# First output stage of a two-block kernel: three of its four pairs by seven block products in place of eight

## The reference, cut to what matters

```
D_MODEL, SEQ, CTX_LEN = 1024, 512, 256          # float32 throughout

def hybrid_layer(x, ctx, mod, mod_c, rot, params, need_ctx_out):
    ...
    rw_l, _ = rwkv_branch(...)                   # [1, 512, 512], recurrent half
    ...
    o = block_attention(q, ...)
    mla_l = o * jax.nn.silu(g_mla)               # [1, 512, 512], attention half
    x = x + gate * (jnp.concatenate([rw_l, mla_l], axis=-1) @ w_out)     # 512x1024 @ 1024x1024
    ...

def first_block(...):
    ...
        x, ctx = hybrid_layer(...)
    return rms_norm(x, final_g)
```

## Time and profile before

| what | us |
|---|---|
| three timed executions | 2710.06, 2714.54, 2714.43 |
| their median | 2714.43 |
| the profiled execution | 2711.91 |
| its span | 2710.1 |
| TensorE busy in the span | 2577.2 (95%) |
| VectorE busy | 1684.0 (62%) |
| ScalarE busy | 948.3 (35%) |
| GpSimd busy | 841.4 (31%) |
| the stage, from its first matmul to the next stage's first | 745.39 to 826.73 |

### The profile page before, as it was taken

How to read it: one execution, slowest core, us unless ns; L and a number is a source line. 1 busy time by engine, 2 the same in 40 slices (tenths; PEclk the granted TensorE clock), 3 DMA queues, 4 the chain that set the end, 5 groups by cost and what they waited for, 6 DMA issues and landing times. The chain is left out here.

```text
span 2710.1 us, 59371 instructions
## 1 busy us (share of the span) xinstructions
PE 2577.2 (95%) x24556; PEld 2048.3 (76%) x24556; DVE 1684.0 (62%) x3037; ACT 948.3 (35%) x2174; POOL 841.4 (31%) x1083
## 2 busy tenths in 40 slices
PE   7989999999999999999999989999999899999998
PEld 5977788775645888867788867767888677858886
DVE  5656767764527837764652358659833776577675
ACT  2013424324422226632121259231212675122571
POOL 3323434330024510012233125236531444246010
PEclk9999999999999999999999999999999999999999
DMA  6331100112431114203101161121111311122200
GB/s 247 98 110 43 45 19 3 51 37 94 157 116 54 63 46 158 95 1 111 62 33 63 63 230 40 76 85 63 42 53 63 140 64 63 63 85 94 79 2 32
DMA packets 108460, 205.98 MB, mean 76 GB/s; under 512 B 21955, under 2 KB 26194, under 8 KB 107680
## 3 DMA queue, kind: packets, MB, share of 16 engines
q1 hardware_dynamic: 107920, 201.30, 21.3%
q0 software_dynamic: 272, 0.89, 0.1%
HBM read 186.85 MB, written 15.54 MB: 75 GB/s over the span
## 5 line engine op out<-in xcount | busy, mean ns | idle before, releaser
L739 PE MATMUL psum<-weights,h_t 128*128 128x256 f32 x1488 | 354.0, 381 | 5.5 <-ACT early_work L828 5.5
L739 PEld LDWEIGHTS psum<-weights,h_t 128*128 128x128 f32 x1488 | 280.1, 191 | 45.4 <-ACT early_work L828 6.7
L739 PE MATMUL psum<-z_l,x_tiles 128*128 128x256 f32 x816 | 192.8, 379 | 0.5 <-POOL z_l L954 0.5
L1528 DVE TENSOR_REDUCE neg_max<-psum 128x1 f32<-128x768 f32 x160 | 147.1, 955 | 67.1 <-PE psum L1304 57.1
L839 ACT ACTIVATE early_work<-psum 128x512 f32<-128x512 f32 (+1 forms) x80 | 45.0, 566 | 364.1 <-DVE psum L1112 248.0
L739 PEld LDWEIGHTS psum<-z_l,x_tiles 128*128 128x128 f32 x816 | 155.0, 190 | 21.9 <-issue 0.9
L1477 ACT ACTIVATE prob<-psum,neg_max 128x768 f32<-128x768 f32 x128 | 114.2, 897 | 79.2 <-DVE neg_max L1528 79.2
L1112 DVE TENSOR_TENSOR psum<-psum,early_work 128x512 f32<-128x512 f32 x62 | 43.1, 696 | 144.6 <-PE psum L739 144.6
L1600 POOL TENSOR_TENSOR z_l<-z_l,inv_total 128x128 f32<-128x128 f32 x64 | 25.4, 401 | 308.6 <-DVE inv_total L1536 308.6
L739 PE MATMUL psum<-weights,x_tiles 128*128 128x256 f32 x496 | 117.2, 379 | 0.0
L790 PE MATMUL psum<-weights,h_t 128*128 128x512 f32 x256 | 111.5, 593 | 1.2 <-PEq L240 1.2
(11 more groups left out here) (548 smaller groups left out, 6674.2 us busy)
## 6 DMA issues: line engine op xcount, KB each, us to landing
weights<-in_ada_w_dram SPq DMA_DIRECT2D x30, 2048.0 KB, 8.0
weights<-in_a_w_in_dram SPq DMA_DIRECT2D x10, 2048.0 KB, 8.1
weights<-in_b_w_in_dram SPq DMA_DIRECT2D x8, 2048.0 KB, 8.0
weights<-in_c_w_in_dram SPq DMA_DIRECT2D x8, 2048.0 KB, 8.1
weights<-in_w_in_dram SPq DMA_DIRECT2D x6, 2048.0 KB, 8.8
x_aside<-x_tiles SPq DMA_DIRECT2D x24, 512.0 KB, 2.6
x_tiles<-x_aside SPq DMA_DIRECT2D x4, 3072.0 KB, 15.7
weights<-in_a_w_out_dram SPq DMA_DIRECT2D x4, 2048.0 KB, 8.2
```

Of the source, the lines that this page charges most:

```text
L739: last = pe.matmul(dst, lhs[:, k, :], rhs[k // 2][:, k % 2, :], start=k == 0, stop=k == KH - 1)
L1528: dve.tensor_reduce(neg_max[:, i % 4, m:m + 1], score_at(i, m), AX, ALU.max, negate=True)\
```

## The change

The diff, cut. `homes` are the places for the right sums and the partial results; the left sums get a new local buffer.

```
-def out_norm_stage(pr, tiles, m_t, bias_col, g_col, next_bank, columns=False, ctx_2=False):
+def out_norm_stage(pr, tiles, m_t, bias_col, g_col, next_bank, homes, columns=False, ctx_2=False):
...
+    half_pairs = n // 2
+    pairs = [(c, p) for c in range(2) for p in range(half_pairs)]
...
+        left = local("left_sums", [P, half_pairs, 4, KT // 2, P])
+        sevens = out_sevens(pr, tiles, m_t, (left,) + homes)
...TensorE
-            for c in range(2):
-                w = pr.weights.get(pe)
-                for i, t in enumerate(tiles):
...
-                    if c == 0 and 1 <= i <= early:
-                        flip(i - 1)
-                    if c == 1 and i:
-                        flip(early + i - 1)
+            for x, (c, p) in enumerate(pairs):
+                if x == 0:
...                        (two tiles by eight steps of 128x512 each, as before)
+                elif p:
+                    first = early + 2 * p - 2 if c else 2 * p - 2
+                    sevens.products(pe, c, p, w, beside=lambda at: flip(first + at))
+                else:
+                    sevens.products(pe, c, p, w)
...
-                if x == 0:
-                    flip(norms - 1)
+                    if k == (KT // 2 if x else KT - 1):
+                        flip(norms - 2 + x)
...VectorE
+            sevens.left_sums(dve, 1)
...                        (modulation and norm_scale, as before)
+            sevens.right_sums(dve, 0, pr.weights.get(dve, w_next))
+            gate_of(0)
+            gate_of(1)
+            for j in range(early):
+                scale(j)
+            for x, (c, p) in enumerate(pairs[1:]):
+                sevens.early_sum(dve, x)
+                sevens.second_sum(dve, x)
+                if c == 0:
+                    sevens.left_sums(dve, 0)
+                    normed_out(0)
+                elif p:
+                    finish_tile(2 * p - 2)
+                    finish_tile(2 * p - 1)
+                    normed_out(early + 2 * p - 2)
+                sevens.right_late(dve, x)
+                gate_of(2 * x + 2)
+                if c == 0:
+                    normed_out(1)
+                elif p:
+                    normed_out(early + 2 * p - 1)
+                sevens.left_late(dve, x)
+                gate_of(2 * x + 3)
+                if c == 0:
+                    sevens.right_sums(dve, 1, pr.weights.get(dve, w_next + 1))
+            for i in (n - 2, n - 1):
+                finish_tile(i)
+            for i in (n - 2, n - 1):
+                normed_out(early + i)
...first_block
+        places = [early[...][:, size * x:size * x + size] for x in range(6)]
+        places += [kept[:, size * x:size * x + size] for x in range(2)]
+        right = [places[0:4], [None] + places[4:7]]
+        terms = kept[:, size:2 * size].rearrange("p (x n) -> p x n", x=4)
```

More of the change, by code:

```diff
@@ L2314, in out_norm_stage @@
     norms = len(order)
+    half_pairs = n // 2
+    pairs = [(c, p) for c in range(2) for p in range(half_pairs)]
+    products = pr.counter("st_products")
+    w_next = pr.weights.next
     with pr.stage() as (block, local):
@@ L2351, in _ @@
             last.then_inc(*spread.tick())
-            u = 0
-            for c in range(2):
-                w = pr.weights.get(pe)
-                for i, t in enumerate(tiles):
[L2356 to L2362, removed]
-                    if c == 0 and 1 <= i <= early:
-                        flip(i - 1)
-                    if c == 1 and i:
-                        flip(early + i - 1)
-                pr.weights.release(projected.now())
+            for x, (c, p) in enumerate(pairs):
+                if p == 0:
+                    w = pr.weights.get(pe)
+                if x == 0:
+                    for u in range(2):
+                        t = tiles[u]
+                        for k in range(KT):
+                            last = pe.matmul(pr.bank(4 + u), m_t[:, k, P * t:P * t + P], w[:, k, :],
+                                             start=(k == 0), stop=(k == KT - 1))
+                        last.then_inc(*projected.tick())
+                elif p:
[3 more added lines that the diff above has]
+                    sevens.products(pe, c, p, w)
+                if p == half_pairs - 1:
+                    pr.weights.release(products.now())
             w = pr.weights.get(pe)
@@ L2406, in _ @@
                     square_of(j)
[L2407 to L2420, removed]
+            for x, (c, p) in enumerate(pairs[1:]):
+                sevens.take_first(act, x)
+                if x == 0:
+                    for j in range(early):
+                        normed_out(j)
+                if c and p:
+                    for i in (2 * p - 2, 2 * p - 1):
+                        finished_square(i)
+                    for i in (2 * p - 2, 2 * p - 1):
+                        normed_out(early + i)
+            for i in (n - 2, n - 1):
+                finished_square(i)
+            for i in (n - 2, n - 1):
+                normed_out(early + i)
         @block.vector
@@ L2439, in normed_out, with gate_of, finish_tile @@
                 last.then_inc(*normed_v.tick())
+            def gate_of(u):
+                c = u // n
+                dve.wait_ge(*projected.at(u + 1))
+                if u >= 2:
+                    dve.wait_ge(*added.at(u - 1))
+                dve.tensor_tensor(delta[:, u % 2, :], pr.bank(4 + u % 4), gate[:, 0, WCOLS * c:WCOLS * c + WCOLS],
+                                  ALU.mult).then_inc(*gated.tick())
+            def finish_tile(i):
+                t = tiles[i]
+                dve.wait_ge(*fn_rooted.at(i + 1))
+                dve.scalar_tensor_tensor(pr.X[:, t, :], pr.X[:, t, :], fn_root[:, i:i + 1], gain[:, :],
+                                         ALU.mult, ALU.mult).then_inc(*fn_scaled.tick())
+                dve.wait_ge(*fn_scaled.at(i + 1))
+                scale(early + i)
+            sevens.left_sums(dve, 1)
             dve.wait_ge(*gates_copied.at(1))
@@ L2451, in _ @@
             dve.wait_ge(*modulated.at(3))
[L2452 to L2475, removed]
@@ L2476, in _ @@
-            normed_out(norms - 1)
+            sevens.right_sums(dve, 0, pr.weights.get(dve, w_next))
+            gate_of(0)
+            gate_of(1)
+            for j in range(early):
+                scale(j)
+            for x, (c, p) in enumerate(pairs[1:]):
+                sevens.early_sum(dve, x)
[17 more added lines that the diff above has]
+                    sevens.right_sums(dve, 1, pr.weights.get(dve, w_next + 1))
@@ L2927, in first_block @@
         mla_branch(pr, mix_t, latent, (b, lnx, gate_s), kept)
-        out_norm_stage(pr, list(range(XT)), mix_t, PCOL["ada_b_2"], PCOL["norm_g_2"], first_bank("A", UNITS[0]), ctx_2=True)
+        size = KT // 2 * WCOLS // 2
+        places = [early[:, :, :].rearrange("p f n -> p (f n)")[:, size * x:size * x + size] for x in range(6)]
+        places += [kept[:, size * x:size * x + size] for x in range(2)]
+        places = [x.rearrange("p (k n) -> p k n", k=KT // 2) for x in places]
+        right = [places[0:4], [None] + places[4:7]]
+        terms = kept[:, size:2 * size].rearrange("p (x n) -> p x n", x=4)
+        out_norm_stage(pr, list(range(XT)), mix_t, PCOL["ada_b_2"], PCOL["norm_g_2"], first_bank("A", UNITS[0]),
+                       (right, terms), ctx_2=True)
 def shift_stage(pr, us, gate_s, masks, lora_w, ones, lnx, b):
```

7 lines of the change are left out of this document (added).

## The result

The changed kernel takes 2719.33 us (median of 20 runs), the kernel before 2712.74 (20 runs, the first three among them): **6.6 us slower, ratio 1.0023, 95% interval 1.0017 to 1.0030**. The forecast was 6.0 slower. Its range, its sign and its likeliest case (slower by over 0.2%) held, the last by a little: the interval begins at 0.17%.

What follows compares the result with a forecast made beforehand. The stage's end was taken as bound by first gate, four chains and tail, not TensorE's work: 4.1 + 1.7 + 0.2 = +6.0 us, giving 2717.9 or 2720.4 by two bases; 2719.2 taken, range 2712 to 2725.

Steps and rivals of the forecast that it cites:

- likeliest case: Whole kernel: slower by over 0.2%, meaning over 5.4 us; chance 0.56.
- What bounds the stage: Stage's second half: its end is set by the first tile's gate, four finishing chains, and what follows the last scaling.
- TensorE's wait: Before the second seven products' second product: TensorE stands still 775.7 to 781.9, 6.2 us, until VectorE's right sums end.
- First term: Gate of the second half's first tile: comes at 791.9 instead of 782.57, +9.4 us.
- Second term: Four tile-finishing chains, from that half's first gate to the last scaling L2428: 34.2 us in place of 35.1.
- Third term: Behind the last scaling, to the stage's last matmul: scaling, turn and three of eight steps, 4.4 us in place of 8.77.
- Fourth term, the clock: TensorE's granted clock falls to 0.50 after waits: 1.7 us plus 0.2 us lost.
- first fall: Clock drop behind TensorE's 6.2 us idle time at the second seven products: 1.7 us, bounds 0 and 3.4.
- second fall: Possible clock drop in the last seven products, after waits for two turns: 0.2 us, bounds 0 and 1.5.
- Not slower: Rival: right sums end by 775.7, so no wait and no clock loss; -2.1 us, 2710 to 2712.3; 5 in 100.
- The clock does not matter: Rival: low clock falls mostly into idle time or ends soon; +3.8 to +4.5 us, 2716.6 to 2719; 18 in 100.

Runs made afterwards that it cites:

- early right sums: Changed kernel with the second half's four right sums moved between VectorE's first two gate products: stage 78.77 us, time 2708.59 us, ratio 0.9986 to the kernel before.
- finishing by pairs: Changed kernel with the tiles' finishing (adds, roots, squares, scalings) written two tiles at a time: stage 83.73 us, ratio 1.0004 to the kernel before.
- the later add: Changed kernel with GpSimd's add of the fourth tile waiting until the four late right sums are through: stage 85.69 us, ratio 1.0024 to the kernel before.
- the one kept busy: Changed kernel with 50 transposes of the unit matrix on TensorE inside its wait for the right sums: stage 85.21 us, ratio 1.0019 to the kernel before.
- the partner without seven products: Kernel before with tiles finished two at a time and five of the eight last steps ahead of the last turn: stage 78.59 us, ratio 0.9988.

## Why the prediction was right

**What bounds the stage** was the step on which all stood: not TensorE's share of work but the first gate, the four chains and what stands behind the last scaling. It held. The pair of kernels with early right sums and with finishing by pairs moved the stage by 9.31 and 4.35, and together (74.25 against 88.08) by 13.83, the sum within 0.2 us. (The 0.17 between is the low clock, which cost 0.17 more in the kernel with finishing by pairs than in the changed one.)

**TensorE's wait** was predicted at 6.2 us and measured at 6.20, from 781.84, which is 775.74 with 6.10 taken off, against the 775.7 predicted. Its parts held too: the fourth gate at 775.26 (predicted 775.4), the four sums with the add among them 6.5. By starts of products the wait is worth 8.08 - 1.73 = 6.35, and not 6.2: a product of eight instructions shows 1.89 from its first start to its last end but the next one starts 1.73 behind it when nothing waits, and this overlap of 0.16 is lost at a wait.

**First term:** predicted +9.4 by VectorE and TensorE alone; measured 12.35 with the clock, and 12.35 - 2.96 = 9.39 without it. One count on the way to it was wrong and not used in a sum: VectorE has five joining operations for every pair, not six; the sixth, `take_first`, is ScalarE's. The trace has 31 more VectorE instructions than before: 8 left sums, 8 right sums, 3 x 5.

**Second term:** predicted 34.2, measured 33.78. L2443 that meets an add took 1.69, that is 0.94 longer and not the 1.2 I had put, and as predicted it delayed a turn and not the chain.

**Third term:** 4.4 predicted, 4.47 measured.

**Fourth term, the clock, was mis-sized.** I took 1.7 for the first fall, between 0 and 3.4. It cost 2.87 to 2.96, near the upper bound: the low level held through the first product and most of the second, not for one alone. The one case in the trace before that I took as nearest had a wait of 2.59 us and one slow product. The changed kernel and the one with finishing by pairs (6.2 us each) were slow in two, 2.96 and 3.13 us lost; the one with the later add (5.26) in one, 1.5 lost. What sets the length is not shown: each is one profile, and the waits differ by 0.9 us only. The second fall cost nothing that the trace shows: the slow seventh product (819.85 + 2.56) ends with VectorE's copies (821.02 + 1.36), which the next sum has to wait for anyway, and the chain behind it kept its time. I had put 0.2. The Trainium skill, page "TensorE: Matmul & The Clock Gate", section "HAM oscillation — how this bites in real kernels", was cited for the rule that a wait leaves the next burst at the low clock. By that rule, the trace agrees; the run with transposes in the wait confirms it from the other side: 1.00 with the same 8.1 us between the two products, and TensorE not idle in them.

**The rival on the other side** ("Not slower") was priced at -2.1 for a wait of zero; the run that takes the wait away gave -2.57 (78.77). In the changed kernel it had no part; it describes the kernel one edit away. The point from which it turns, a wait of 2.1 us without the clock, was not tried. A slip in another rival, "The clock does not matter": the lower of its two times is 2711.9 + 3.8 = 2715.7, not 2716.6; nothing rests on it.

**The median** came out at 2719.33 for 2719.2 predicted. That is closer than the working deserves: the kernel before had a median of 2712.74 over its twenty runs and 2714.43 in the three first ones, and the difference was 6.6 for 6.0. The 6.0 itself had help from errors that partly cancel: the first fall of the clock was put 1.3 too low, the four chains 0.4 and the second fall 0.2 too high.

## What to carry to other kernels

A trick that saves work on the busiest engine needs its preparation to be ready ahead of the point where that engine asks; on an engine that works in order, look up what stands in front of the preparation and add it up. Here four operations of 1.2 us in the wrong place (one of them held up by an add) cost 6.4 us of waiting and 3 of clock, against 4.9 saved on TensorE, and in the right place, under work that was there anyway, they cost nothing. And when a stage ends in a chain around several engines, read its end as first release, chain and tail: the chain taken two tiles at a time gave 4.35 us without one instruction less.

## What the runs showed of the hardware that was not expected

- A gap of 5.3 to 6.2 us on TensorE was followed by 1.2 GHz in all three kernels that had one idle, for one or two products of 1.73 us (1.5 to 3.1 us lost), and not in the one where 50 transposes of the unit matrix filled it (5.6 us, with 0.75 idle behind them).
- Shorter waits did it too, and not every time. In the last seven products TensorE waits 2.13 us for the first turn. In the kernels with early right sums and with the later add the product right behind that turn already ran slow (3.52 and 3.26 us for 1.89; granted clock 0.51 in the first). In the changed kernel and the one kept busy the same wait left the clock at 1.00, and it fell behind the next one, of 2.98 us, 2.8 us of work later (0.50 at 817.8). In this stage waits of up to 1.6 us in the kernel before, and up to 1.8 in the partner without seven products, left it at 1.00.
- VectorE's scaling of 128x1024 with one input in SBUF (0.75 alone) took 1.69 beside GpSimd's add, as sums of two inputs took 2.17 for 1.22: in both cases 0.94 to 0.95 longer, less than the 1.27 that the add takes alone.
